# Merge stage of a hybrid decoder step: gates and projections as seven quarter products instead of eight

## The chip, the cores and the metric

The kernel runs on one core of a Trainium2 chip. The metric is the device time of one execution in microseconds. Everything is float32.

## The reference, cut to what matters

The program is one step of a decoder trunk with two branches, RWKV-7 time mixing and sparse attention, over 1024 prompt tokens and 8 sample tokens. The change concerns how the two branches are merged:

```
zs, zg_r, q, ..., zg_n, mg = split_in(rmsnorm(h, norm_g) @ w_in)      # mg: 2 x 1024 columns
g_r, g_n = split(sigmoid(mg), 2)
m = g_r * ((o_r * silu(zg_r)) @ proj_r) + g_n * ((o_n * silu(zg_n)) @ proj_n)   # proj_*: 512 x 1024
h = h + m @ w_out                                                     # w_out: 1024 x 1024
e = rmsnorm(p @ w_pe, pe_norm_g)
h = h + sigmoid(h @ w_pg) * e
```

## The kernel before, in words

Stages follow each other in one program, each with a queue of instructions written out by hand for each engine (SyncE issues the loads); semaphores order them, and a stage begins when all engines have ended the one before.

Activations lie transposed in on-chip memory, features on the 128 partitions and the 1032 tokens (TT, 1024 prompt and 8 sample) along the row: `xnT` (8 blocks of 128 features, the normalized input), `zgr` and `zgn` (4 blocks each, parts of `zT`, the gated outputs of the two branches), `mT` (8 blocks, the merged result). When the merge stage begins, `mT` holds the first gate g_r, which earlier stages computed between their own matmuls. Such a stage, `attend_sample`, also issues the first two loads of merge weights.

`merge_branches` goes over 8 blocks f of 128 output features and, in each, over three thirds of 344 tokens (CG): 24 units u. A unit has 16 matmuls on TensorE: 8 for the second gate (line 2666, weights `wm` from w_in, moving operand `xnT`), 4 for each projection (line 2670, weights `wp`). ScalarE takes the sigmoid of the gate (L2680), VectorE multiplies each projection with its gate from PSUM (L2690), GpSimd adds the two into `mT` (L2707). Two sets of PSUM banks alternate. SyncE loads the weights of block f + 2 (one load of 512 KB, one of 256, two of 128) when block f is summed, and behind the first of these the 4 MB of `w_out`. After units 15, 17 and 19 VectorE makes sums of w_out's quarters (`w_sums`, L2694 to L2700).

`finish_tokens`, the last stage, computes m @ w_out and h @ w_pg for pairs of token tiles, already each as seven products of quarters (P1 to P7, in the order P1, P5, P6, P2, P7, P3, P4) for eight. A product is 4 float32 matmuls of 512 columns (L2823). The operand sums of the tokens (`sums`, in `ring_k`) and of the weights are VectorE's work. The stage opens with `sample_out` (L2907), 64 narrow records of the 8 sample tokens; behind it come the seven products of pair 0. The residual additions (L3131) read a product from PSUM, and P6, P7 and P4 wait for the additions before them, since they add into the same bank.

Of the kernel before, what the change touches and what calls it, by code (L numbers as in the profile page):

```python
# [14 lines left out]
ALU = mybir.AluOpType  # L15
# [2185 lines left out]
def load_merge_weights(sp, k, x, f):  # L2201

    s, cols = f % 2, slice(f * P, (f + 1) * P)
    w_rows = x.w_in[0].rearrange("(c p) n -> p c n", p=P)
    r_rows = x.proj_r[0].rearrange("(c p) n -> p c n", p=P)
    n_rows = x.proj_n[0].rearrange("(g j d) n -> g d j n", g=2, d=HD)
    sp.dma_start(k.wm[:, s], w_rows[:, :, OFF_MGN + f * P:OFF_MGN + (f + 1) * P]).then_inc(k.in_merge_w[s], 16)
    sp.dma_start(k.wp[:, s, 0], r_rows[:, :, cols]).then_inc(k.in_merge_w[s], 16)
    for g in range(2):
        sp.dma_start(k.wp[g * HD:(g + 1) * HD, s, 1], n_rows[g, :, :, cols]).then_inc(k.in_merge_w[s], 16)  # L2210


def attend_sample(nc, k, x):
# [5 lines left out]
    with Stage(nc) as ctx:  # L2219
# [57 lines left out]
        def _(sp):  # L2277
# [16 lines left out]
            for f in range(2):  # L2294
                load_merge_weights(sp, k, x, f)
# [335 lines left out]
def merge_branches(nc, k, x):  # L2631

    ring = 2
    with Stage(nc) as ctx:
        wm, wp, in_w = k.wm, k.wp, k.in_merge_w
        free = k.zT[:, 8:10, :].rearrange("p a t -> p (a t)")
        sg = free[:, 0:2 * CG].rearrange("p (s t) -> p s t", s=2)
        tt = free[:, 2 * CG:6 * CG].rearrange("p (s n t) -> p s n t", s=2, n=2)  # L2640
        in_wo = ctx.sem("in_w_out")
        summed, sigd, termed, added, made = (ctx.sem(n) for n in ("m_summed", "m_sig", "m_terms", "m_added", "w_out_sums"))
        block = ctx.enter_context(nc.Block())
        lo, hi, left, right = slice(0, 4), slice(4, 8), slice(0, 512), slice(512, D)

        @block.sync
        def _(sp):
            for f in range(ring, KC):
                sp.wait_ge(summed, 3 * (f - ring + 1))
                load_merge_weights(sp, k, x, f)  # L2650
                if f == ring:
                    sp.dma_start(k.w_out[:], x.w_out[0].rearrange("(c p) n -> p c n", p=P)).then_inc(in_wo, 16)
            sp.wait_ge(in_wo, 16)

        @block.tensor
        def _(pe):
            for f in range(KC):
                s = f % ring
                pe.wait_ge(in_w[s], 64 * (f // ring + 1))
                for g in range(3):  # L2660
                    u, cs = 3 * f + g, slice(g * CG, (g + 1) * CG)
                    b = 4 * (u % 2)
                    if u >= 2:
                        pe.wait_ge(termed, 2 * (u - 1))
                    for c in range(KC):
                        nc.tensor.matmul(k.ps[:, b + 1, 0:CG], wm[:, s, c, :], k.xnT[:, c, cs],  # L2666
                                         start=(c == 0), stop=(c == KC - 1))
                    for n, src in enumerate((k.zgr, k.zgn)):
                        for c in range(NPAIR):
                            last = nc.tensor.matmul(k.ps[:, b + 2 + n, 0:CG], wp[:, s, n, c, :], src[:, c, cs],  # L2670
                                                    start=(c == 0), stop=(c == NPAIR - 1))
                    last.then_inc(summed, 1)

        @block.scalar
        def _(act):
            for u in range(3 * KC):
                act.wait_ge(summed, u + 1)
                if u >= 2:
                    act.wait_ge(termed, 2 * (u - 1))
                nc.scalar.activation(sg[:, u % 2], k.ps[:, 4 * (u % 2) + 1, 0:CG], ACT.Sigmoid).then_inc(sigd, 1)  # L2680

        @block.vector
        def _(dve):
            for u in range(3 * KC):
                dve.wait_ge(sigd, u + 1)
                if u >= 2:
                    dve.wait_ge(added, u - 1)
                gates = (k.mT[:, u // 3, u % 3 * CG:(u % 3 + 1) * CG], sg[:, u % 2, :])
                for n in range(2):
                    nc.vector.tensor_tensor(tt[:, u % 2, n, :], k.ps[:, 4 * (u % 2) + 2 + n, 0:CG], gates[n],  # L2690
                                            ALU.mult).then_inc(termed, 1)
                if u == 15:
                    dve.wait_ge(in_wo, 16)
                    nc.vector.tensor_tensor(k.wt[:, 0], k.w_out[:, lo, right], k.w_out[:, lo, left], ALU.subtract).then_inc(made, 1)  # L2694
                if u == 17:
                    dve.wait_ge(made, 1)
                    nc.vector.tensor_tensor(k.wt[:, 1], k.w_out[:, hi, right], k.wt[:, 0], ALU.subtract).then_inc(made, 1)
                if u == 19:
                    dve.wait_ge(made, 2)
                    nc.vector.tensor_tensor(k.wt[:, 2], k.w_out[:, hi, left], k.wt[:, 1], ALU.subtract).then_inc(made, 1)  # L2700

        @block.gpsimd
        def _(pool):
            for u in range(3 * KC):
                f, g = u // 3, u % 3
                pool.wait_ge(termed, 2 * (u + 1))
                nc.gpsimd.tensor_tensor(k.mT[:, f, g * CG:(g + 1) * CG], tt[:, u % 2, 0, :], tt[:, u % 2, 1, :],  # L2707
                                        ALU.add).then_inc(added, 1)


PRODUCTS = ("P1", "P5", "P6", "P2", "P7", "P3", "P4")


def finish_tokens(nc, k, x, o):
# [8 lines left out]
    with Stage(nc) as ctx:  # L2723
# [3 lines left out]
        wo, wot, wg, we = k.w_out, k.wt, sb("w_pg", [P, KC, D]), sb("w_pe", [P, 2, D])  # L2727
# [20 lines left out]
        s_made, t3_made, tg_made = ctx.sem("operand_sums"), ctx.sem("w_out_t3"), ctx.sem("w_pg_sums")  # L2748
# [70 lines left out]
        def _(pe):  # L2819
# [7 lines left out]
            def out_product(name, p):  # L2827
                if name == "P1" and p >= 2:
                    pe.wait_ge(h_out, 7 * (p - 1))
                elif name == "P5":  # L2830
                    pe.wait_ge(s_made, 4 * p + 1)
                    if p:
                        pe.wait_ge(h_out, 7 * p - 1)
                elif name == "P6":
                    pe.wait_ge(s_made, 4 * p + 2)
                    pe.wait_ge(h_out, 7 * p + 1)
                elif name == "P7":
                    pe.wait_ge(s_made, 4 * p + 3)
                    pe.wait_ge(h_out, 7 * p + 3)
                    pe.wait_ge(t3_made, 1)  # L2840
                elif name == "P3":
                    pe.wait_ge(s_made, 4 * p + 4)
                elif name == "P4":
                    pe.wait_ge(h_out, 7 * p + 5)
                product(name, p).then_inc(h_ps, 1)
# [261 lines left out]
        def _(dve):  # L3107
# [57 lines left out]
            def sums_of_gate_weights(n):  # L3165
                if n == 0:
                    nc.vector.tensor_tensor(wot[:, 0], wg[:, 0:4, cols(1)], wg[:, 0:4, cols(0)], ALU.subtract).then_inc(tg_made, 1)
                elif n == 1:
                    dve.wait_ge(tg_made, 1)
                    nc.vector.tensor_tensor(wot[:, 1], wg[:, 4:8, cols(1)], wot[:, 0], ALU.subtract).then_inc(tg_made, 1)  # L3170
                elif n == 2:
                    dve.wait_ge(tg_made, 2)
# [218 lines left out]
```

## Time and profile before

| | us |
|---|---|
| runs of the kernel before | 1857.47, 1858.22, 1869.94 |
| median | 1858.22 |
| profiled execution, its time | 1855.13 |
| its span, first to last instruction | 1853.0 |
| mean granted TensorE clock, share of full | 0.974 |
| merge stage, TensorE's first to last record | 1370.04 to 1594.05 |

Times in the trace are microseconds from the start of the span. PE is TensorE's matmuls, PEld its weight loads (they overlap PE), DVE VectorE, ACT ScalarE, POOL GpSimd, SP SyncE; PEq and SPq are sequencers. A float32 matmul stands as two records. L2666 is line 2666 of the kernel.

### The profile page before, as it was taken

Reading aid. Unit: us, or ns where it says so; the run is one execution under the profiler, and the core shown is the slowest. Engines: PE = TensorE matmul, PEld = TensorE weight load, DVE = VectorE, ACT = ScalarE, POOL = GpSimd, SP = SyncE. Lnnn points to the kernel's source line nnn. Section 1 sums busy time; section 2 is a strip of 40 time slices with the busy share of each in tenths; the row PEclk is TensorE's granted clock in tenths of the full one; section 3 lists DMA queues with packets and bytes.
Section 4 is the critical chain, followed back from the end, with each engine's and each line's share of the span. In section 5 each row is a group of like instructions: output and inputs, shape, how many; then the busy total and the mean of one; then the engine's idle time right before and its main releaser. Section 6 shows DMA issues by size and latency. Waiting matters only on the chain. (4 is left out here: it accounts for less than half of the span.)

```text
span 1853.0 us, 40230 instructions
## 1 busy us (share of the span) xinstructions
PE 1729.4 (93%) x17720; PEld 1141.5 (62%) x17720; DVE 750.0 (40%) x1520; ACT 545.7 (29%) x1145; POOL 385.6 (21%) x438
## 2 busy tenths in 40 slices
PE   7999899999999899799888599899999999999997
PEld 5666566666666555666666489776656666545443
DVE  3101255555554262366666566172111111323444
ACT  4111344344432101465666021222310000011344
POOL 0111232222221000154444321112200011000112
PEclk9999899999999999799999799999999999999999
DMA  4111000000001161460000597538624010410001
GB/s 153 46 35 51 2 14 15 14 17 23 14 14 26 51 119 23 115 171 1 2 2 1 224 288 264 181 99 198 151 46 136 23 46 23 179 72 1 23 23 45
DMA packets 115026, 135.82 MB, mean 73 GB/s; under 512 B 48204, under 2 KB 97045, under 8 KB 110286
## 3 DMA queue, kind: packets, MB, share of 16 engines
q1 hardware_dynamic: 105536, 83.95, 16.3%
q0 software_dynamic: 9216, 49.29, 8.6%
q8 instruction: 140, 2.29, 0.5%
q14 instruction: 32, 0.26, 0.0%
q10 hardware_dynamic: 102, 0.03, 0.0%
HBM read 120.64 MB, written 16.62 MB: 74 GB/s over the span
## 5 line engine op out<-in xcount | busy, mean ns | idle before, releaser
L725 PE MATMUL ps<-xnT,rw_side_w 128*128 128x344 f32 x576 | 204.5, 479 | 0.0
L443 PE MATMUL ps<-xnT,w_z 128*128 128x344 f32 x624 | 184.2, 457 | 2.3 <-DVE xnT L537 1.3
L443 PEld LDWEIGHTS ps<-xnT,w_z 128*128 128x128 f32 x624 | 119.3, 192 | 63.9 <-issue 3.3
L1928 POOL TENSOR_SCALAR probs<-probs,row_sums,gates 128x63 f32<-128x63 f32 (+6 forms) x148 | 95.0, 657 | 260.7 <-DVE row_sums L1888 260.7
L725 PEld LDWEIGHTS ps<-xnT,rw_side_w 128*128 128x128 f32 x576 | 99.5, 191 | 40.4 <-issue 3.6
L2180 PE MATMUL ps<-xnT,zT 128*128 128x344 f32 x384 | 121.4, 465 | 0.0
L2666 PE MATMUL ps<-xnT,ring_k 128*128 128x344 f32 x384 | 116.7, 458 | 2.2 <-PEq L81 2.2
L2670 PE MATMUL ps<-zT,ring_k 128*128 128x344 f32 x384 | 115.0, 452 | 0.0
L2666 PEld LDWEIGHTS ps<-xnT,ring_k 128*128 128x128 f32 x384 | 73.8, 192 | 41.2 <-issue 4.0
L2670 PEld LDWEIGHTS ps<-zT,ring_k 128*128 128x128 f32 x384 | 73.0, 190 | 38.0
L2180 PEld LDWEIGHTS ps<-xnT,zT 128*128 128x128 f32 x384 | 72.1, 195 | 36.2 <-issue 6.0
L256 PE MATMUL ps<-w_kv,xnT 128*128 128x396 f32 x256 | 89.0, 510 | 4.6 <-DMA w_kv<-in_w_in_dram 4.6
L2690 DVE TENSOR_TENSOR zT<-ps,mT 128x344 f32<-128x344 f32 x24 | 12.4, 516 | 197.7 <-ACT zT L2680 197.7
L1797 PE MATMUL ps<-ident,probs 128*128 128x128 f32 (+1 forms) x460 | 70.4, 283 | 20.1 <-ACT probsT L1853 11.1
L1837 ACT ACTIVATE probs<-probs,neg_max 128x63 f32<-128x63 f32 (+6 forms) x148 | 87.5, 595 | 3.3 <-DVE neg_max L1878 3.3
L2707 POOL TENSOR_TENSOR mT<-zT 128x344 f32<-128x344 f32 x24 | 27.9, 1161 | 244.1 <-DVE zT L2690 244.1
L256 PEld LDWEIGHTS ps<-w_kv,xnT 128*128 128x128 f32 x256 | 49.4, 194 | 43.9 <-DMA w_kv<-in_w_in_dram 8.9
L1784 PE MATMUL ps<-kT,zT 64*128 64x512 f32 (+3 forms) x384 | 73.8, 497 | 2.4 <-PEq L81 1.1
L1853 ACT ACTIVATE probsT<-ps 128x512 f32<-128x512 f32 (+1 forms) x80 | 45.9, 574 | 100.7 <-PE ps L1797 100.2
L2680 ACT ACTIVATE zT<-ps 128x344 f32<-128x344 f32 x24 | 11.0, 457 | 215.3 <-PE ps L2670 215.3
L1797 PEld LDWEIGHTS ps<-ident,probs 128*128 128x128 f32 (+1 forms) x460 | 50.7, 142 | 35.3 <-issue 17.4
L1811 PE MATMUL ps<-probsT,kvtok 128*64 128x128 f32 x1056 | 71.8, 281 | 0.5 <-ACT probsT L1853 0.5
(531 smaller groups left out, 3000.0 us busy)
## 6 DMA issues: line engine op xcount, KB each, us to landing
w_z<-in_w_in_dram SPq DMA_DIRECT2D x13, 512.0 KB, 3.7
xnT_kept<-xnT SPq DMA_DIRECT2D x1, 4128.0 KB
xnT<-xnT_kept SPq DMA_DIRECT2D x1, 4128.0 KB, 13.6
x_tok<-in_x_prompt_dram SPq DMA_DIRECT2D x8, 512.0 KB, 5.7
rw_side_w<-in_w_in_dram SPq DMA_DIRECT2D x16, 256.0 KB, 3.3
zT<-in_w_in_dram SPq DMA_DIRECT2D x8, 512.0 KB, 5.9
ring_k<-in_w_in_dram SPq DMA_DIRECT2D x8, 512.0 KB, 3.9
w_out<-in_w_out_dram SPq DMA_DIRECT2D x1, 4096.0 KB
```

The source lines that it names most:

```text
L256: last = nc.tensor.matmul(k.ps[:, u % 4, 0:half], k.xnT[:, c, i * P:(i + 1) * P], w[:, c, h * half:(h + 1) * half], start=(c == 0), stop=( ...
L443: last = nc.tensor.matmul(k.ps[:, u % 6, 0:CG], w[:, n % w_ring, c, :], k.xnT[:, c, g * CG:(g + 1) * CG], start=(c == 0), stop=(c == KC - 1))
L725: ins = nc.tensor.matmul(k.ps[:, SIDE_BANKS[g % 2], 0:CG], w.side[:, t % 2, c, :], k.xnT[:, c, g % 3 * CG:(g % 3 + 1) * CG], start=(c == 0 ...
L1784: last = nc.tensor.matmul(k.ps[:, 2 * (s % 2) + g, at:at + w], k.qT[half(g), j, i * P:(i + 1) * P], keys[half(g), t0:t0 + w], start=True, ...
L1797: last = nc.tensor.transpose(k.ps[0:m, 4 + pc % 2, (2 * b + g) * P:(2 * b + g + 1) * P], region(n, br, g, t * P, m), k.ident[:])
L1811: last = nc.tensor.matmul(k.ps[half(g), 6 + n % 2, 0:P], vals, pt[0:m, pc % NPT, (2 * b + g) * P:(2 * b + g + 1) * P], start=(br == 1 and ...
L1837: nc.scalar.activation(every, every, ACT.Exp, scale=-1.0, bias=neg_m[:, at:at + 1], accum_out=ls[:, at:at + 1]).then_inc(expd, 1)
L1853: nc.scalar.activation(to, src, ACT.Copy).then_inc(pt_a, 1)
L1928: nc.gpsimd.tensor_scalar(every, every, ls[:, at:at + 1], k.gates[:, i, gate:gate + 1], ALU.mult, ALU.mult).then_inc(scaled, 1)
L2180: ins = self.nc.tensor.matmul(self.k.ps[:, self.banks[n % nb], 0:CG], self.w[:, t % 2, c, :], self.k.xnT[:, c, g * CG:(g + 1) * CG], start ...
L2666: nc.tensor.matmul(k.ps[:, b + 1, 0:CG], wm[:, s, c, :], k.xnT[:, c, cs], start=(c == 0), stop=(c == KC - 1))
L2670: last = nc.tensor.matmul(k.ps[:, b + 2 + n, 0:CG], wp[:, s, n, c, :], src[:, c, cs], start=(c == 0), stop=(c == NPAIR - 1))
```

## The change

The merge stage is split in two by time, and both parts use quarters.

- Gates first, for all features: four units, one for each pair of feature blocks (p, p + 4). Input features, output features and tokens are each cut in two: of the inputs 4 blocks and 4 blocks, of the outputs block p and block p + 4, and of the tokens each half of 516 into two quarters of CQ = 258. Seven products of quarters stand for eight; each is 4 matmuls of 258 columns, and is made for both token halves i. This is one round r of 14 product groups.
- Then both projections: four units of two rounds (n = 0: proj_r, n = 1: proj_n), each again 7 products for both halves, but with 2 matmuls in each, since a projection has 4 input blocks.
- The second gates are kept, in a new buffer `gate_n` of 7 blocks and a free place in `zT`; a projection's results are multiplied in place with `mT` (n = 0) or `gate_n` (n = 1), and GpSimd adds the two in the rounds n = 1.
- ScalarE copies three intermediate sums of each round from PSUM (`held`), VectorE adds them to the later products; ScalarE takes the sigmoids in the gate rounds.
- VectorE makes the sums of weights (`operand_sum`, 4 of 512 columns a unit), of inputs (`input_sum`, 4 of 2064 columns, before the first round) and of the branches (`branch_sums`, 8 of 1032 columns in the fourth round).
- Weights load in pairs of blocks, 1 MB a unit. `w_out`, whose memory holds the input sums, is loaded only after the gate rounds.
- The three sums of w_out move from the merge stage to the last stage, where the buffer `w_sums` now lives; with the fourth, which was there already, they are made in order: two before sample_out is awaited, one behind it, one after P6's residual of pair 0.

```
+CQ = TT // 4
+MERGE_UNITS, GATE_UNITS = 8, 4
+MERGE_ROUNDS = GATE_UNITS + 2 * (MERGE_UNITS - GATE_UNITS)
...
+            for u in range(2, MERGE_UNITS):
+                sp.wait_ge(summed, 14 * (last_round(u - 2) + 1))
+                load_merge_pair(sp, k, x, u)
+                if u == GATE_UNITS + 1:
+                    sp.wait_ge(summed, 14 * GATE_UNITS)
                     sp.dma_start(k.w_out[:], x.w_out[0].rearrange("(c p) n -> p c n", p=P)).then_inc(in_wo, 16)
...
         @block.tensor
+            for r in range(MERGE_ROUNDS):
+                u, n = unit_of(r)
+                if n == 0:
+                    pe.wait_ge(in_w[u % 2], merge_landed(u))
+                for name in PRODUCTS:
+                    for i in range(2):
+                        bank = {"P2": 4 + i, "P5": 6 + i, "P3": 6 + i}.get(name, bank_a(r, i))
+                        if name == "P1":
+                            if 2 <= r < GATE_UNITS + 2:
+                                pe.wait_ge(sigd, 8 * (r - 2) + 7 + i)
+                            elif r >= GATE_UNITS + 2:
+                                pe.wait_ge(gated, 8 * (r - 2 - GATE_UNITS) + 7 + i)
+                        elif name == "P5":
+                            pe.wait_ge(s_made, 4 * u + 1)
+                            pe.wait_ge(tx_made if r < GATE_UNITS else tz_made, 1 if r < GATE_UNITS else 2)
+                            if r:
+                                pe.wait_ge(added, 6 * (r - 1) + 5 + i)
...
+                        else:
+                            pe.wait_ge(tx_made if r < GATE_UNITS else tz_made, 4 if r < GATE_UNITS else 8)
+                            pe.wait_ge(added, 6 * r + 3 + i)
+                        tiles = 4 if u < GATE_UNITS else 2
+                        for c in range(tiles):
+                            last = nc.tensor.matmul(k.ps[:, bank, 0:CQ], stationary(u, n, name, c), moving(u, n, name, c, i),
+                                                    start=(c == 0 and name in ("P1", "P5", "P2")), stop=(c == tiles - 1),
+                                                    skip_group_check=True)
+                        last.then_inc(summed, 1)
...
         @block.scalar
+                for b, bank in enumerate((bank_a(r, 0), 6, bank_a(r, 0))):
+                    for i in range(2):
+                        act.wait_ge(summed, 14 * r + 2 * b + i + 1)
...
+                        nc.scalar.activation(held[:, b, i, :], k.ps[:, bank + i, 0:CQ], ACT.Copy).then_inc(copied, 1)
...
         @block.vector
+            def finished(r, b):
+                u, n = unit_of(r)
+                j, h = ((0, 0), (1, 1), (0, 1), (1, 0))[b]
+                for i in range(2):
+                    dve.wait_ge(summed, 14 * r + (7, 9, 11, 13)[b] + i)
+                    f, q = u % 4 + 4 * j, held[:, min(b, 2), i, :]
+                    part = k.ps[:, (4 + i, bank_a(r, i), 6 + i, bank_a(r, i))[b], 0:CQ]
+                    gate = k.mT[:, f, columns(i, h)] if n == 0 else gate_block(f, i, h)
+                    if b < 3:
+                        dve.wait_ge(copied, 6 * r + (1, 3, 5)[b] + i)
+                        to = q if r >= GATE_UNITS else gate_block(f, i, h)
+                        nc.vector.tensor_tensor(to, part, q, ALU.add).then_inc(added, 1)
+                        part = q
+                        if r >= GATE_UNITS:
+                            dve.wait_ge(added, 6 * r + 2 * b + i + 1)
+                    if r >= GATE_UNITS:
...
+                        nc.vector.tensor_tensor(gate, part, gate, ALU.mult).then_inc(gated, 1)
...
+            for r in range(MERGE_ROUNDS):
+                u, n = unit_of(r)
+                more = r == last_round(u) and u + 1 < MERGE_UNITS
+                if r == GATE_UNITS - 1:
+                    branch_sums(0, 2, 0)
+                    branch_sums(2, 2, 2)
+                finished(r, 0)
+                if r == GATE_UNITS - 1:
+                    branch_sums(1, 8, 2)
+                if more:
+                    operand_sum(u + 1, 0)
+                    operand_sum(u + 1, 1)
+                finished(r, 1)
...
         @block.gpsimd
+            for r in range(GATE_UNITS + 1, MERGE_ROUNDS, 2):
+                u, n = unit_of(r)
+                for b, (j, h) in enumerate(((0, 0), (1, 1), (0, 1), (1, 0))):
+                    for i in range(2):
+                        f = u % 4 + 4 * j
+                        pool.wait_ge(gated, 8 * (r - GATE_UNITS) + 2 * b + i + 1)
+                        to = k.mT[:, f, columns(i, h)]
+                        nc.gpsimd.tensor_tensor(to, to, gate_block(f, i, h), ALU.add).then_inc(joined, 1)
...
 def finish_tokens(nc, k, x, o):
             operand_sums(0)
+            weight_sums(wo, 0, to_made)
+            weight_sums(wo, 1, to_made)
             dve.wait_ge(sh_ps, 1)
-            nc.vector.tensor_tensor(wo[:, 0:4, cols(1)], wo[:, 4:8, cols(1)], wo[:, 0:4, cols(1)], ALU.subtract).then_inc(t3_made, 1)
+            weight_sums(wo, 2, to_made)
...
                 residual(p, 3, 0, 1, a, True)
+                if p == 0:
+                    weight_sums(wo, 3, to_made)
```

## Rows read from the trace of the kernel before

**Rows 1.** The page's summary: busy us, share of the span and instructions by engine.
```profile
PE 1729.4 (93%) x17720; PEld 1141.5 (62%) x17720; DVE 750.0 (40%) x1520; ACT 545.7 (29%) x1145; POOL 385.6 (21%) x438
```

**Rows 2.** TensorE in time, merge stage: start, length, records, idle before.
```profile
1370.04 6.56 PE L2666 MATMUL ps<-xnT,ring_k 128*128 128x344 f32 x16 [2.18 <-PEq L81]
...
1381.06 4.79 PE L2666 MATMUL ps<-xnT,ring_k 128*128 128x344 f32 x16
...
1589.26 4.79 PE L2670 MATMUL ps<-zT,ring_k 128*128 128x344 f32 x16
```

**Rows 3.** Stretches: engines' busy time, then granted clock, DMA share, GB/s.
```profile
1370.00:1594.00 224.00, 223.97 (x768) 146.86 (x768) 28.17 (x49) 10.51 (x23) 26.95 (x23) 0.99 0.17 47
...
1370.00:1376.00 6.00, 5.96 (x15) 3.76 (x16) 0.00 (x0) 0.00 (x0) 0.00 (x0) 0.72 0.01 4
...
1594.00:1600.00 6.00, 2.76 (x29) 1.53 (x32) 3.01 (x8) 0.46 (x1) 1.44 (x5) 0.72 0.03 10
```

**Rows 4.** TensorE in time, last stage.
```profile
1597.28 5.02 PE L2907 MATMUL ps<-w_out,mT 128*32 128x256 f32 x64 [3.24 <-PEq L81]
...
1605.77 7.03 PE L2823 MATMUL ps<-w_sums,ring_k 128*128 128x512 f32 x16
...
1625.27 3.60 PE L2823 MATMUL ps<-w_sums,mT 128*128 128x512 f32 x8
...
1723.53 3.60 PE L2823 MATMUL ps<-w_pg,mT 128*128 128x512 f32 x8
...
1747.57 3.60 PE L2823 MATMUL ps<-w_sums,ring_k 128*128 128x512 f32 x8
1752.17 3.67 PE L2823 MATMUL ps<-w_sums,ring_k 128*128 128x512 f32 x8 [1.01 <-ACT w_out L3003]
```

**Rows 5.** TensorE in time, small matmuls with full weights.
```profile
1252.97 1.00 PE L2395 MATMUL ps<-s_win,ones 128*128 128x64 f32 x8
```

**Rows 6.** All engines in time, merge stage.
```profile
1521.40 2.28 DVE L2694 TENSOR_TENSOR w_sums<-w_out 128x2048 f32<-128x2048 f32 x1
1521.56 2.89 POOL L2707 TENSOR_TENSOR mT<-zT 128x344 f32<-128x344 f32 x1 [8.34 <-DVE zT L2690]
...
1594.57 0.52 DVE L2690 TENSOR_TENSOR zT<-ps,mT 128x344 f32<-128x344 f32 x1 [8.32 <-ACT zT L2680]
...
1595.59 0.91 POOL L2707 TENSOR_TENSOR mT<-zT 128x344 f32<-128x344 f32 x1 [8.34 <-DVE zT L2690]
```

**Rows 7.** VectorE in time, start of the last stage.
```profile
1599.41 0.68 DVE L3118 TENSOR_TENSOR ring_k<-mT 128x512 f32<-128x512 f32 x1
1600.02 0.68 DVE L3120 TENSOR_TENSOR ring_k<-ring_k,mT 128x512 f32<-128x512 f32 x1
1600.73 0.69 DVE L3122 TENSOR_TENSOR ring_k<-mT,ring_k 128x512 f32<-128x512 f32 x1
1602.36 2.29 DVE L3184 TENSOR_TENSOR w_out<-w_out 128x2048 f32<-128x2048 f32 x1 [0.94 <-PE ps L2907]
...
1605.97 0.69 DVE L3131 TENSOR_TENSOR h_tok<-ps,h_tok 128x512 f32<-128x512 f32 x1 [0.98 <-PE ps L2823]
...
1616.27 0.69 DVE L3131 TENSOR_TENSOR h_tok<-ps,h_tok 128x512 f32<-128x512 f32 x1 [2.74 <-PE ps L2823]
```

**Rows 8.** ScalarE and GpSimd in time, 256 columns, last stage.
```profile
1629.93 0.38 ACT L3055 ACTIVATE squares_s<-ps 128x256 f32<-128x256 f32 x1 [10.09 <-PE ps L2934]
...
1659.12 0.73 POOL L3094 TENSOR_TENSOR y_sample<-y_sample,g_pe_s 128x256 f32<-128x256 f32 x1 [61.35 <-DVE y_sample L3216]
```

**Rows 9.** DMA in 1390 to 1430: GB/s in 40 slices, issues and landing.
```profile
GB/s 0 0 0 0 0 0 0 0 0 0 18 263 331 294 235 342 414 401 401 426 410 418 377 414 410 90 16 0 0 0 0 0 0 0 0 0 0 0 49 287
...
ring_k<-in_w_in_dram SPq DMA_DIRECT2D x2, 512.0 KB, 3.9
```

**Rows 10.** VectorE in time, 512 columns beside additions of GpSimd.
```profile
1742.85 1.64 DVE L3154 TENSOR_TENSOR h_tok<-w_out,h_tok 128x512 f32<-128x512 f32 x1
1744.96 1.21 DVE L3152 TENSOR_TENSOR w_out<-w_out 128x512 f32<-128x512 f32 x1 [0.47 <-ACT w_out L3022]
```

More of the change, by code:

```diff
@@ new lines, in gate_block, with weights, sums_of @@
+        def gate_block(f, i, h):
+            tile = gate_n[:, f, :] if f < KC - 1 else place[:, 0:TT]
+            return tile[:, columns(i, h)]
+        def weights(u, j, half):
+            if u < GATE_UNITS:
+                return wq[:, u % 2, j, 4 * half:4 * half + 4, :]
+            return wq[:, u % 2, j].rearrange("p (n c) m -> p n c m", n=2)[:, :, 2 * half:2 * half + 2, :]
+        def sums_of(u, q):
+            if u < GATE_UNITS:
+                return sums[:, q, :].rearrange("p (c m) -> p c m", m=P)
+            return sums[:, q, :].rearrange("p (n c m) -> p n c m", n=2, m=P)
@@ new lines, in branch_sum, with branch, stationary @@
+        def branch_sum(q, n):
+            rows = slice(2 * n, 2 * n + 2)
+            return (xv[:, rows, :, 0, :], xv[:, 4 + 2 * n:6 + 2 * n, :, 0, :], zv[:, 4 * n:4 * n + 2, :, 1, :],
+                    xv[:, rows, :, 1, :])[q]
+        def branch(n, half, h):
+            return zv[:, 4 * n + 2 * half:4 * n + 2 * half + 2, :, h, :]
+        def stationary(u, n, name, c):
+            j, half = {"P1": (0, 0), "P2": (0, 1), "P4": (1, 1)}.get(name, (None, None))
+            if j is None:
+                q = {"P5": 0, "P6": 1, "P7": 2, "P3": 3}[name]
+                at = (c if u < GATE_UNITS else 2 * n + c) * P
+                return sums[:, q, at:at + P]
+            return wq[:, u % 2, j, 4 * half + c if u < GATE_UNITS else 4 * n + 2 * half + c, :]
@@ L2682, in _, with operand_sum @@
         @block.vector
         def _(dve):
[L2684 to L2688, printed above, removed]
-                for n in range(2):
[L2690 to L2700, printed above, removed]
+            def operand_sum(u, q):
+                if q == 0:
+                    dve.wait_ge(in_w[u % 2], merge_landed(u))
+                if u:
+                    dve.wait_ge(summed, 14 * last_round(u - 1) + (4, 6, 10, 12)[q])
+                if q == 1 or q == 3:
+                    dve.wait_ge(s_made, 4 * u + q - (q == 3))
+                one, other, op = ((weights(u, 1, 0), weights(u, 1, 1), ALU.add), (sums_of(u, 0), weights(u, 0, 0), ALU.subtract),
+                                  (weights(u, 0, 0), weights(u, 1, 0), ALU.subtract),
+                                  (weights(u, 0, 1), sums_of(u, 1), ALU.subtract))[q]
+                nc.vector.tensor_tensor(sums_of(u, q), one, other, op).then_inc(s_made, 1)
@@ new lines, in _ @@
+            for q in range(4):
+                operand_sum(0, q)
+                input_sum(q)
+            for r in range(MERGE_ROUNDS):
+                u, n = unit_of(r)
[10 more added lines that the diff above has]
+                finished(r, 1)
+                if r == GATE_UNITS - 1:
+                    branch_sums(3, 10, 6)
+                if more:
+                    operand_sum(u + 1, 2)
+                finished(r, 2)
+                if more:
+                    operand_sum(u + 1, 3)
+                if r >= GATE_UNITS:
+                    finished(r, 3)
```

176 lines of the change are left out of this document (105 added, 71 removed).

## The prediction, made before the changed kernel ran

> **What bounds the kernel now.** I read the summary first: TensorE has work for 93% of the span, no other engine for more than 40% [rows 1]. Then the matmul timeline of the merge stage [rows 2]: after a slow start the blocks of 16 records follow each other every 4.63 us, with no idle note, until the last block ends at 1589.26 + 4.79 = 1594.05. The table by stretches says the same, 223.97 us busy in 224.00, while VectorE works 28.2 us, ScalarE 10.5 and GpSimd 27.0 [rows 3]. So the stage is as long as its matmul stream, and helpers matter only where TensorE has to wait for them. A float32 matmul leaves two records. From 1381.06 to 1589.26 lie 45 blocks of 16, 208.20 us / 720 = 289.2 ns per record of 344 columns.
>
> **What a record of 258 columns takes.** The trace has none. Records of 512 columns stand 429.3 ns apart (1723.53 to 1747.57, 56 records) [rows 4]. Between 344 and 512 that is 140.1 / 168 = 0.834 ns per column, two passes at the 2.4 GHz level, with 2.5 ns left over. 258 columns: 289.2 - 86 x 0.834 = 217.5 ns. This holds only if the weight load still hides. A load shows as 190 ns, of full weights, but 8 records of 64 columns with fresh 128x128 weights fit in 1.00 us, 125 ns each at most [rows 5]. That is the nearest row to a floor, and it is well below 217.5. I take 217.5; ends 216 and 222.
>
> **The matmul sum.** Before: 24 units (8 feature blocks, 3 token thirds) of 16 matmuls, 768 records, 222.1 us. After: four gate rounds of 7 products x 2 halves x 4 tiles are 224 matmuls, eight projection rounds of 7 x 2 x 2 are 224 more; 896 records x 217.5 = 194.9 us. **Term 1: -27.2 us.** (12.5% fewer columns; the fixed 2.5 ns per record is paid 128 times more often, 0.3 us.)
>
> **The start of the stage.** The first 16 records took 6.56 us, later ones 4.79 [rows 2], at a granted clock of 0.72 [rows 3]; the idle before them was 2.18 us. This 1.8 us stays. New in front of it are VectorE's sums: four of 512 columns and four of 2064, in turn. By rows of 0.69 us (0.61 start to start when nothing is waited for, 0.71 when the one before is) and 2.28 for 2048 [rows 6, 7], P5's operands are there at 0.7 + 2.3 = 3.0, P6's at 6.1, P7's at 9.0 and P4's at 12.1. TensorE asks for them at 3.5 to 5.3, 8.8, 15.7 and 22.7 (each product 16 x 217.5 = 3.48, plus the slow start). Nothing is paid; cover 0.5 us at worst.
>
> **Gate rounds (24.4 us each).** VectorE has 6 additions from PSUM. A 344-column one is 0.516, a 512-column one 0.69 [rows 6, 7], so 258 columns are about 0.43; with four weight sums, 5.3 us a round. P7's half is ready at 15.7, P4 of that half wants its bank back at 20.9. ScalarE's six copies (0.38 each by a 256-column row [rows 8]) and eight sigmoids of that size make 5.3 us of 24.4, and the sigmoids are wanted only two rounds later. In the fourth round come eight branch sums of 1032 columns, 1.23 each: four between 3.5 and 8.4, two from 13.9, with two weight sums and P7's addition after them at 18.4 against 20.9 needed; then two more and the rest until 23.5, before P5 of the next round wants anything at 26.1. Nothing is paid. DMA: as before 1 MB per pair of blocks, asked for a whole unit (24.4 us) ahead, where a landing takes 3.9 us; w_out (4 MB) moves from the first third to the middle, about 97 us before it is needed, and took some 15 us (slices 11 to 25, of 1 us) [rows 9]. What is queued behind the later wait on SyncE is only the next pair, not due before another 24 us. Nothing.
>
> **Projection rounds (56 records, 12.2 us each).** Here product and half are two matmuls, 0.87 us, and the margins shrink. Counted from the round's start, P2 halves end at 6.1 and 7.0, P7 at 7.8 and 8.7; P4 wants its banks at 10.4 and 11.3, which needs the additions of P7. VectorE from 7.0 on: add 0.43, multiply 0.41, in the second round of a unit two sums of the next weights (1.3), then P7's first add, done near 9.6. Margin 0.8 us. P5 of the next round (13.9, 14.8) needs P3's additions, done near 12 and 13. Without further trouble nothing is paid.
>
> The further trouble is GpSimd. In the second round of each unit it adds eight pairs of 258 columns, both in SBUF, just while VectorE multiplies and sums SBUF by SBUF. The trace shows that these hold each other up: a GpSimd addition of 344 columns is 0.91 alone but 2.89 when it is issued 0.16 us into VectorE's 2048-column sum, and it ends 0.77 after that sum [rows 6]. It works the other way too: VectorE's 512-column additions take 1.21 to 1.64 instead of 0.69 beside GpSimd [rows 10]. A GpSimd addition of 258 columns is about 0.73 [rows 8]. One of them falling between 7.0 and 10.4 uses the margin, two overrun it by 0.7. Three rounds (the second ones of the first three units) have both kinds of work, so between 0 and, with the same again at P5, 3 x 1.4 = 4.2 us. Most orders of arrival give one such wait before P7's addition. **Term 2: +1.0 us (0 to 4.2).**
>
> The Trainium skill has this as a rule ("SBUF — State Buffer", the section on the two separate sides): the port pair of VectorE and GpSimd is an exclusive lock for a whole instruction, also taken by a VectorE operation with two SBUF inputs. By that rule, the trace agrees in both directions; it turns the margin of a mean into one of an order, and it is what rival B prices from the rows.
>
> **The end of the stage.** Before: sigmoid, two products, GpSimd's sum of 0.91; from the last matmul's end (1594.05) to the next stage's first (1597.28) 3.24 us, of which 0.78 after GpSimd [rows 4, 6]. After: one multiply from PSUM (0.47 with its wait) and the sum (0.08 + 0.73), so 1.3 + 0.8 = 2.1 at the least. GpSimd comes with a backlog: eight sums become due between 7.0 and 12.7, and each can be held 0.41 by a multiply; at 1.14 each until VectorE falls silent it is done about 2.5 after the last matmul, 3.3 in all. I take 2.8. **Term 3: -0.4 us (-1.1 to +0.5).**
>
> **The last stage.** It inherits four sums of 2048 columns; one (L3184) was there already. VectorE now does the two first ones after its operand sums (1601.3 on): 1603.6 and 1605.9; the third, which must wait for sample_out's end at 1602.3, ends at 1608.2 instead of 1604.65; behind it stand the h_sample addition (256 columns, about 0.4) and the first residual, which ends at 1609.2 instead of 1606.66 [rows 7]. P5 (1605.77) has what it needs since 1603.6. P6 would start at 1609.2 (1605.77 + 8 x 0.429) [rows 4] and waits for that residual: 0 to 0.2 us. The fourth sum falls into the idle 2.7 us ahead of 1616.27 and is not wanted before P4, at 1625 [rows 4, 7]. Removed from the merge stage, the three sums save nothing, since they stood beside matmuls. **Term 4: +0.1 us (0 to 1).**
>
> **Sum.** -27.2 + 1.0 - 0.4 + 0.1 = -26.5. The profiled execution took 1855.13 (span 1853.00 and 2.1 around it), so 1828.6 for a profiled one. The median of the three runs is 1858.22, 3.1 above; the forecast is 1858.22 - 26.5, about 1831.7. About 1% (18.6 us) is what a measurement here can tell from no change; faster by more ends at 1839.6.
>
> **Rivals.**
> A, my forecast: dense stream, terms as above. Terms 2 to 4 at their good ends give -28.3 (1829.9), record ends of 216 ns another 1.3; all bad ends -21.5. Chance 0.68, own range 1827 to 1835.
>
> B: the hold-ups between VectorE and GpSimd decide the projection rounds. If every sum of GpSimd costs VectorE its full 0.73, a second round holds 8 x 0.43 + 6 x 0.41 + 4 x 0.65 + 8 x 0.73 = 14.3 us for VectorE, against 12.2 of matmuls: +2.1 in four rounds, 8.4, with the end at +0.5 and the last stage at +0.5. -27.2 + 9.4 = -17.8, 1840.4. For it: the held operations of [rows 6, 10]. Against: half of VectorE's operations read PSUM and were not held in any row here, and the first rounds, with 5.9 us of VectorE work, take up arrears. Chance 0.17, 1835 to 1843.
>
> C, slower: TensorE's clock. After an idle of 2.18 us the next 6 us ran at 0.72, and 0.72 again after 3.24 [rows 2, 3]; after 1.01 us in the last stage eight records took 3.67 against 3.60 [rows 4]. Should P4 in each of twelve rounds wait over 2 us for VectorE's additions, each time costs 2.2 of waiting and 1.8 of slow records, 48 us: -27 + 48 = +21, 1879. It decides from waits of about 2 us on, in more than half of the rounds; at my margins (0.8) waits of 0.7 are in sight, not 2. Chance 0.05.
>
> D: many short groups cost TensorE something. There are 112 groups of four records with up to three waits each. In the last stage groups of eight with up to three waits run at the plain 429 ns [rows 4], no row has groups of four. 0.05 us each would give +5.6, 1837; 0.25 each would eat the gain, 1859. Chance 0.07, 1837 to 1859.
>
> E: it does not do what it says, because something else was the limit of the stage, a load for example. The stream without idle [rows 2] speaks against it; 0.03, about 1855.
>
> Range for 8 in 10: A and most of B, 1827 to 1841. Faster by over 1%: A, three quarters of B, under half of D, 0.68 + 0.13 + 0.03 = 0.84. Within 1%: the rest of B, half of D, and E, 0.11. Slower: C, 0.05.
>
> **What the new profile would show.** Record spacing in the stage of 217.5 ns, blocks of eight records 1.74 us apart (217 right; 250 or more: the load does not hide, and term 1 is wrong). The first P5 without an idle note. In projection rounds, idle of TensorE put down to VectorE ahead of P4 or P5, in rounds 5, 7 and 9 only (term 2), under 1 us each; in all rounds, B or C. VectorE multiplies and GpSimd sums above 0.41 and 0.73 where they overlap. The gap from the last merge matmul to sample_out between 2.1 and 3.3. P6 of the first output pair at most 0.2 late, P4 on time. A granted clock below 0.95 anywhere inside the stage but at its start would make the prediction wrong, and so would a first P1 held by its loads.

## The result, and the profile after

The changed kernel took 1828.26 us, the median of 4 runs (1827.45 to 1845.88), against 1861.76 of 4 runs of the kernel before (1857.47 to 1869.94). The ratio is 0.9852, with a 95% interval from 0.9811 to 0.9892: faster by 1.5%. Timed again on another occasion (last experiment), 1836.05 of 6 runs stand against 1857.12 of 11, ratio 0.9894, from 0.9861 to 0.9927. The two intervals overlap, and neither holds 1. The forecast started from 1858.22, the median of three of the four runs of the kernel before. The profiled execution took 1828.42 us, its span is 1826.6.

First the summary and the slices of the changed kernel's page; the slices show where in the span an engine is busy, in tenths.

```profile
PE 1701.3 (93%) x17848; PEld 1164.6 (64%) x17848; DVE 825.5 (45%) x1652; ACT 575.4 (32%) x1225; POOL 384.3 (21%) x446
...
PEld 5666566666666645566666388876668888545443
```

Beside [rows 1], matmuls are busy 28.1 us less in spite of 128 more instructions, weight loads 23 us more, VectorE 75.5 more, ScalarE 29.7 more. In the slices of the merge stage weight loads stand at 8 tenths (before at 6). The helpers' work cost nothing where they had time.

TensorE in time, from the merge stage's start into the last stage; it answers to [rows 2, 4]. What stands in brackets is called the idle note: how long the engine sat idle before these records, and what ended it.

```profile
1370.08 5.41 PE L2766 MATMUL ps<-xnT,ring_k 128*128 128x258 f32 x16 [2.18 <-PEq L81]
1375.32 7.12 PE L2766 MATMUL ps<-w_out,zT 128*128 128x258 f32 x32
...
1469.28 1.90 PE L2766 MATMUL ps<-zT,ring_k 128*128 128x258 f32 x8
1471.02 3.64 PE L2766 MATMUL ps<-xnT,zT 128*128 128x258 f32 x16
...
1488.42 3.64 PE L2766 MATMUL ps<-zT 128*128 128x258 f32 x16
1491.97 1.98 PE L2766 MATMUL ps<-xnT,ring_k 128*128 128x258 f32 x8
1493.78 1.90 PE L2766 MATMUL ps<-zT,ring_k 128*128 128x258 f32 x8
...
1565.39 1.90 PE L2766 MATMUL ps<-xnT,ring_k 128*128 128x258 f32 x8
1570.59 3.66 PE L3082 MATMUL ps<-w_out,mT 128*32 128x256 f32 x64 [3.29 <-PEq L81]
...
1577.72 3.60 PE L2995 MATMUL ps<-w_sums,ring_k 128*128 128x512 f32 x8
1582.73 3.67 PE L2995 MATMUL ps<-w_sums,ring_k 128*128 128x512 f32 x8 [1.42 <-DVE h_tok L3306]
```

Four things are to be seen. From 1375.32 to 1469.28 lie 27 blocks of 16 with no idle note: 3.48 us each, 217.5 ns per record. The first block, 5.41 for 3.64, shows the slow start, 1.8 us as before. P4 of round 5 starts at 1491.97, 0.07 after it would follow (1488.42 + 3.48), and its block takes 1.81 us instead of 1.74. And idle notes stand only ahead of the last stage (3.29) and, new, at P6 of pair 0, released by VectorE's L3306; it is 1.58 us late (1577.72 + 3.43 = 1581.15). An idle note counts from the modelled end of the record before and so shows 1.42. The stage's stretch and the last stage's first 3.59 us, by busy time and granted clock, answer to [rows 3]:

```profile
1370.08:1567.29 197.21, 197.21 (x896) 170.88 (x896) 97.03 (x178) 40.64 (x104) 24.36 (x29) 0.99 0.18 54
```

```profile
1570.59:1574.18 3.59, 3.59 (x64) 2.36 (x65) 2.91 (x8) 0.00 (x0) 0.49 (x4) 1.00 0.26 46
```

The way to compare the two profiles is by stage, since executions differ before the change begins: TensorE's first merge record stands at 1370.04 before and 1370.08 here, but between 1373.5 and 1381.9 in the eight other profiles of the changed kernel or a variant of it, whose code up to there is the same. So the whole time carries up to 12 us that arise before the stage; from the merge stage's start to the end the changed kernel's two profiles agree to 0.1 us (456.52, and 456.59 in the last experiment). Of the kernel before there is one profile, so whether it reaches the stage at another time on average is not shown.

| us | before | after | difference |
|---|---|---|---|
| merge stage, first to last record | 224.01 | 197.21 | -26.80 |
| from there to sample_out | 3.23 | 3.30 | +0.07 |
| last stage to the end | 255.72 | 256.01 | +0.29 |
| sum | 482.96 | 456.52 | -26.44 |

One difference in it is not the change's for certain: `sample_out`, with which the last stage opens, took 4.95 us before (1597.28 [rows 4] to 1602.23) at a granted clock of 0.72, and 3.59 after at 1.00. At the full clock the profile of the kernel before would be up to 1.36 us shorter, and the sum could shrink to -25.1 from -26.4 (an estimate from these two durations).

### The profile page after: what moved, and what is told of

It reads as the page before. It is cut to its first block and busy times, and to the rows that moved or that the text cites. A ratio compares the mean times of both kernels' runs of the same rounds, so it can differ in the third digit from the quotient of the medians.

```text
span 1826.6 us, 40926 instructions
## 1 busy us (share of the span) xinstructions
PE 1701.3 (93%) x17848; PEld 1164.6 (64%) x17848; DVE 825.5 (45%) x1652; ACT 575.4 (32%) x1225; POOL 384.3 (21%) x446
## 5 line engine op out<-in xcount | busy, mean ns | idle before, releaser
L562 DVE SCALAR_TENSOR_TENSOR zT<-z_diff,vec,zT 128x1032 f32<-128x1032 f32 x13 | 16.8, 1293 | 126.2 <-POOL z_diff L417 113.5
L1811 PEld LDWEIGHTS ps<-probsT,kvtok 128*64 128x64 f32 x1056 | 57.1, 138 | 21.5 <-issue 19.6
L1909 DVE COPY probsT<-ps 128x512 f32<-128x512 f32 (+1 forms) x80 | 50.7, 634 | 44.4 <-PE ps L1797 44.4
L2883 POOL TENSOR_TENSOR mT<-mT,gate_n 128x258 f32<-128x258 f32 x28 | 23.7, 852 | 218.0 <-DVE gate_n L2846 218.0
L1224 POOL TENSOR_TENSOR rw_Lb<-rw_Lm,level_mask 128x512 f32<-128x512 f32 x40 | 53.9, 1357 | 62.4 <-DVE rw_Lm L1393 38.8
L2782 ACT ACTIVATE zT<-ps 128x258 f32<-128x258 f32 x72 | 27.8, 386 | 109.0 <-PE ps L2766 86.3
L2995 PE MATMUL ps<-w_sums,ring_k 128*128 128x512 f32 x128 | 57.3, 595 | 4.5 <-ACT w_out L3178 3.0
```

The lines of the kernel that those rows point to most:

```text
L1224: nc.gpsimd.tensor_tensor(w.Lb[:, n % 2], w.Lm[:].rearrange("p q c n -> p (q c) n"), bc(k.tab["level_mask"][:, n + 1, :], 1, 8), ALU.mult) ...
L1811: last = nc.tensor.matmul(k.ps[half(g), 6 + n % 2, 0:P], vals, pt[0:m, pc % NPT, (2 * b + g) * P:(2 * b + g + 1) * P], start=(br == 1 and ...
L1909: nc.vector.tensor_copy(to, src).then_inc(pt_v, 1)
L2995: last = nc.tensor.matmul(k.ps[:, bank, :], left[:, c, :], right[:, c, :], start=(first and c == 0), stop=(c == 3), skip_group_check=True)
```

## The experiments

### The missing eighth put back

```
-                        for c in range(tiles):
+                        for c in [c for _ in range(2 if name == "P2" else 1) for c in range(tiles)]:
```

> The changed kernel with the product P2 issued twice in every round, the second time over the first, so that every round has eight products; all helper work, the order of gates and projections and the loads are those of the changed kernel. Theory (the gain is the missing eighth of the matmul stream): 64 matmuls and so 128 records more, 128 x 217.5 ns = 27.8 us; the profiled time goes from 1828.4 to about 1856.2, within 1 us of the kernel before (1855.1), and the merge stage from 197.2 to 225.0 us. Rival (a part of the gain comes from gates before projections, smaller tiles or the moved sums): the time ends more than 3 us below that of the kernel before. Rival 2 (helpers bind in the projection rounds): the longer rounds hide something, and less than 25 us is added.

Measured: 1859.52 (10 runs) against 1859.69 (13 runs) of the kernel before, ratio 0.999, from 0.997 to 1.0011. The profiled execution took 1861.32 and not the expected 1856.2; it reached the stage 5.7 us later than the changed kernel's, so the stage decides. TensorE in time, its start and the start of the next:

```profile
1375.79 5.41 PE L2766 MATMUL ps<-xnT,ring_k 128*128 128x258 f32 x16 [2.18 <-PEq L81]
...
1603.52 3.66 PE L3082 MATMUL ps<-w_out,mT 128*32 128x256 f32 x64 [3.08 <-PEq L81]
```

The stage took 224.64 us (1375.79 to 1603.52 less the gap of 3.08), 27.43 more than without the eighth product; from its start to the end 483.71, against 482.96 before. The 128 records more would be 27.84 us at 217.5 ns; 0.41 is missing because P4 does not wait in this run (term 2 below). With eight products the whole change is worth +0.75 us: that is the price of its helpers, shorter matmuls, moved sums. Of it 0.63 lies in the stage, where 1024 records of 217.5 ns for 768 of 289.2 make 0.6; against a profile of the kernel before at the full clock in sample_out the price would be up to 2.1 (the same estimate). Both rivals fall. This is the cleanest evidence of where the gain comes from: not from gates before projections, nor from smaller tiles, but from an eighth of the stream.

### The third sum of w_out later

```
-            dve.wait_ge(sh_ps, 1)
-            weight_sums(wo, 2, to_made)
             for p in range(NPR):
                 residual(p, 1, 0, 0, a, True)
+                if p == 0:
+                    dve.wait_ge(sh_ps, 1)
+                    weight_sums(wo, 2, to_made)
```

(and the h_sample addition with it)

> The changed kernel, but VectorE makes the third sum of w_out (and the h_sample addition) after the first residual of pair 0 instead of before it. Theory (in the last stage P6 waits 1.42 us for that residual, which stands behind three sums of 2048 columns): the wait at P6 goes, P6 starts at P5's start + 3.43, and everything behind it comes 1.4 us earlier, unless the clock is down at the stage's start, when there was no such wait to begin with and the gain is 0.2. Rival (the next in line is as late: the load of p for the small transposes, or P7, whose operand is this third sum): the wait only moves to the transposes after P2 or to P7, and nothing is gained.

VectorE in time, in the changed kernel and then in this one:

```profile
1574.65 2.28 DVE L3347 TENSOR_TENSOR w_sums<-w_out 128x2048 f32<-128x2048 f32 x1
1576.96 2.29 DVE L3347 TENSOR_TENSOR w_sums<-w_out,w_sums 128x2048 f32<-128x2048 f32 x1
1579.36 2.29 DVE L3347 TENSOR_TENSOR w_out<-w_out 128x2048 f32<-128x2048 f32 x1
...
1581.91 0.68 DVE L3306 TENSOR_TENSOR h_tok<-ps,h_tok 128x512 f32<-128x512 f32 x1
```

```profile
1590.99 0.68 DVE L3306 TENSOR_TENSOR h_tok<-ps,h_tok 128x512 f32<-128x512 f32 x1
1591.59 2.28 DVE L3347 TENSOR_TENSOR w_out<-w_out 128x2048 f32<-128x2048 f32 x1
```

TensorE in this one, whose P5 and P6 are one block again:

```profile
1582.40 3.66 PE L3082 MATMUL ps<-w_out,mT 128*32 128x256 f32 x64 [3.29 <-PEq L81]
...
1589.53 7.03 PE L2995 MATMUL ps<-w_sums,ring_k 128*128 128x512 f32 x16
1596.39 3.60 PE L2995 MATMUL ps<-w_out,mT 128*128 128x512 f32 x8
```

The residual that P6 waits for ends 9.27 us after the stage's start instead of 12.00, the wait at P6 is gone, and nothing takes its place: transposes and P7 follow without an idle note. The last stage takes 254.40 instead of 256.01. The theory holds, the rival doesn't. The median of this kernel, 1837.61 against 1859.69 (ratio 0.9883, from 0.9858 to 0.9909), shows nothing of this, because this execution reached the merge stage 11.8 us later than the changed kernel's: an effect of 1.6 us is to be read from the stage.

### GpSimd's additions left out, and made twice

Out in rounds 5, 7 and 9:

```
-            for r in range(GATE_UNITS + 1, MERGE_ROUNDS, 2):
+            for r in range(MERGE_ROUNDS - 1, MERGE_ROUNDS, 2):
```

> The changed kernel without GpSimd's additions in rounds 5, 7 and 9 (three quarters of the merged result lack the second branch); only the last unit is added. Theory (a GpSimd addition and a VectorE operation with two on-chip-memory inputs hold each other): in rounds 5, 7 and 9 the second weight sum falls from 1.03 to 0.69 us, multiplies from 0.66-0.73 to 0.43, and the idle of 0.07 us ahead of P4 goes; the merge stage is 0.2 us shorter. Rival (the durations are of dependence on the operation before, or of PSUM access): they stay as they are.

Twice (with a semaphore between the two):

```
+                        nc.gpsimd.tensor_tensor(place[:, TT + 6 * CQ:TT + 7 * CQ], to, gate_block(f, i, h), ALU.add).then_inc(twice, 1)
                         nc.gpsimd.tensor_tensor(to, to, gate_block(f, i, h), ALU.add).then_inc(joined, 1)
```

> The changed kernel with each of GpSimd's additions made twice, the first into a scratch place. Theory (hold-ups by GpSimd are what eats VectorE's margin ahead of P4): twice as many operations of 0.73 us between 7.0 and 10.4 us of the odd projection rounds hold VectorE longer, and P4 waits 0.3 to 1.5 us in rounds 5, 7 and 9 instead of 0.07; the end of the stage comes some 3 to 6 us later, since GpSimd's sixteen additions of the last round take at least 11.7 us from about 7 us on. Rival (each VectorE operation is held at most once, by the one GpSimd operation in progress, and GpSimd was already busy there): the wait ahead of P4 stays under 0.3 us and only the end of the stage moves.

Each of the two ran once; they are read from the stage and from durations, not from their whole times (1838.07 and 1840.17).

All engines in time, the changed kernel, round 5 around P4:

```profile
1489.67 0.68 DVE L2807 TENSOR_TENSOR zT<-ring_k 128x512 f32<-128x512 f32 x1
1489.82 1.11 POOL L2883 TENSOR_TENSOR mT<-mT,gate_n 128x258 f32<-128x258 f32 x1 [0.36 <-DVE gate_n L2846]
1490.45 1.03 DVE L2807 TENSOR_TENSOR zT<-zT,ring_k 128x512 f32<-128x512 f32 x1
1491.41 0.41 DVE L2839 TENSOR_TENSOR zT<-ps,zT 128x258 f32<-128x258 f32 x1
...
1491.97 1.98 PE L2766 MATMUL ps<-xnT,ring_k 128*128 128x258 f32 x8
```

The same place on VectorE without GpSimd:

```profile
1498.38 0.68 DVE L2807 TENSOR_TENSOR zT<-ring_k 128x512 f32<-128x512 f32 x1
1499.17 0.69 DVE L2807 TENSOR_TENSOR zT<-zT,ring_k 128x512 f32<-128x512 f32 x1
1499.78 0.42 DVE L2839 TENSOR_TENSOR zT<-ps,zT 128x258 f32<-128x258 f32 x1
```

And with the additions made twice, VectorE and then TensorE:

```profile
1493.75 1.21 DVE L2808 TENSOR_TENSOR zT<-ring_k 128x512 f32<-128x512 f32 x1
1495.07 1.03 DVE L2808 TENSOR_TENSOR zT<-zT,ring_k 128x512 f32<-128x512 f32 x1
1496.03 0.41 DVE L2840 TENSOR_TENSOR zT<-ps,zT 128x258 f32<-128x258 f32 x1
```

```profile
1496.59 1.98 PE L2767 MATMUL ps<-xnT,ring_k 128*128 128x258 f32 x8 [0.43 <-DVE zT L2840]
...
1521.62 1.98 PE L2767 MATMUL ps<-xnT,ring_k 128*128 128x258 f32 x8 [0.43 <-DVE zT L2840]
...
1546.65 1.98 PE L2767 MATMUL ps<-xnT,ring_k 128*128 128x258 f32 x8 [0.43 <-DVE zT L2840]
...
1581.29 6.37 PE L3085 MATMUL ps<-w_out,mT 128*32 128x256 f32 x64 [8.30 <-PEq L81]
```

Read the durations: the second weight sum takes 1.03, 0.69, 1.03 us, the first one 0.68, 0.68, 1.21, while additions from PSUM stay at 0.41 to 0.43 in all three. P7's first addition ends at 1491.82 in the changed kernel, P4 would be due at 1491.90 and starts at 1491.97, 0.15 after that addition's end (in the run with the additions made twice it is 0.15 too, 1496.44 to 1496.59). With the longer block behind it that is 0.13 to 0.14 us in each of three rounds, 0.41. Without GpSimd in these rounds the stage takes 196.80 us, 0.41 less than 197.21: the whole of it, and twice the 0.2 that was expected. With twice its work P4 is 0.60 late each time (idle notes of 0.43) and the stage takes 198.82, and GpSimd's sixteen additions of the last round hold the next stage back to 8.30 us after the last matmul. The mechanism is shown from both sides; its size is small, since two additions of GpSimd held a multiply by 0.23 (0.66 us for 0.43) and a weight sum by 0.34, while VectorE without them was done 0.65 ahead of P4 (1500.20 against 1500.85).

### Fewer columns

```
+                            w = CQ if c == 0 and name in ("P1", "P5", "P2") else 129
-                            last = nc.tensor.matmul(k.ps[:, bank, 0:CQ], stationary(...), moving(...),
+                            last = nc.tensor.matmul(k.ps[:, bank, 0:w], stationary(...), moving(...)[:, 0:w],
```

> The changed kernel, in which every merge matmul but the first of P1, P5 and P2 of each half has 129 columns instead of 258 (half of each quarter of tokens gets only a part of its sum). One size is changed, to ask what holds a record when the columns no longer do. Theory (the two passes over the columns set the spacing, the weight load hides): 129 x 0.834 + 2.5 = 110 ns between narrow records; a gate round falls from 24.4 to 12 x 217.5 + 100 x 110 ns = 13.6 us. Rival (the weight load of 190 ns becomes the limit): 190 ns or more, a gate round of 21.6 us. In the projection rounds the matmuls fall to 7.5 us, while VectorE's work there was 6.5 us in a first round and 9.5 in a second one: there the stage becomes VectorE's, P4 waits in every second round, and the pair of rounds takes 16 to 18 us instead of 24.4.

The other with 64 in the place of 129:

> As the run with 129 columns, with 64. Theory (columns alone): 64 x 0.834 + 2.5 = 56 ns between narrow records. Rival (a floor of the weight load, of the rows with 64 columns of the kernel before at most 125 ns): 100 to 125 ns, the same in a gate round as with 129 columns.

Both leave out a part of the sums, and each ran once. TensorE in time with 129 columns, a gate round, then projection rounds:

```profile
1393.34 2.37 PE L2767 MATMUL ps<-xnT,ring_k 128*128 128x258 f32 x16
...
1401.76 3.74 PE L2767 MATMUL ps<-xnT,zT 128*128 128x129 f32 x32
1405.33 1.95 PE L2767 MATMUL ps<-w_out,ring_k 128*128 128x129 f32 x16
1407.12 2.37 PE L2767 MATMUL ps<-xnT,ring_k 128*128 128x258 f32 x16
...
1449.43 1.95 PE L2767 MATMUL ps<-zT 128*128 128x129 f32 x16
1453.19 1.48 PE L2767 MATMUL ps<-xnT,ring_k 128*128 128x129 f32 x8 [1.81 <-DVE zT L2840]
...
1471.23 1.48 PE L2767 MATMUL ps<-xnT,ring_k 128*128 128x129 f32 x8 [1.80 <-DVE zT L2840]
```

With 64 columns:

```profile
1388.79 7.03 PE L2767 MATMUL ps<-xnT,zT 128*128 128x64 f32 x32
...
1414.43 2.37 PE L2767 MATMUL ps<-xnT,ring_k 128*128 128x258 f32 x16
...
1422.85 3.74 PE L2767 MATMUL ps<-xnT,zT 128*128 128x64 f32 x32
1426.42 1.95 PE L2767 MATMUL ps<-w_out,ring_k 128*128 128x64 f32 x16
1428.21 2.37 PE L2767 MATMUL ps<-xnT,ring_k 128*128 128x258 f32 x16
```

Narrow records stand (1405.33 - 1401.76) / 32 = 111.6 ns apart with 129 columns, and (1426.42 - 1422.85) / 32 = 111.6 with 64; gate rounds last 13.78 us in both. So 64 columns gain nothing over 129, as the rival for 64 said: that is the floor with fresh full weights, 111.6 ns, although a load shows as 190. At 129 columns theory (110) and floor meet; 258 are far above it. In the projection rounds P4 waits 1.8 us in every second round and a pair takes 18.04 us (1453.19 to 1471.23), just above the expected 16 to 18: there the stage is VectorE's. In the run with 64 columns the blocks from 1376.80 to 1402.86 ran at a granted clock of 0.50 to 0.52, the lower of the two levels (7.03 us for 32 records against 3.74), with no idle note among them, and three places in the projection rounds at 0.59 to 0.67. Its stage took 145.52 us against 129.89 with 129 columns, where the clock was 0.99 from 1380.93 to 1430, and its whole time, 1782.47, is above 1771.48. The spacing of 111.6 ns is read where the clock was 1.00; why it stayed low is open.

### Three edits of order together, beside the changed kernel again

The third sum late, as above; and

```
                 if more:
                     operand_sum(u + 1, 0)
-                    operand_sum(u + 1, 1)
+                    if r < GATE_UNITS:
+                        operand_sum(u + 1, 1)
                 finished(r, 1)
+                if more and r >= GATE_UNITS:
+                    operand_sum(u + 1, 1)
```

and the last round's two additions of P4's results on VectorE instead of GpSimd.

> The changed kernel with three edits of order: the third sum of w_out after the first residual (as in the run with the late third sum, 1.6 us less from the last stage's start to the end), the second weight sum of a unit after P7's additions instead of before them in the projection rounds (takes away the 0.07 us ahead of P4 in three rounds, 0.2 us), and in the last round the additions of P4's halves on VectorE instead of GpSimd (GpSimd ended 2.5 us after the last matmul, VectorE 1.0; by the durations 1.9 for both, 0.5 us less). Theory: 2.3 us less than the changed kernel from the merge stage's start to the end, 456.5 to 454.2. Rival (the end of the stage is bound by VectorE and GpSimd holding each other, so that moving two additions gains nothing): 454.7 to 455. The whole time differs by several us between executions before the merge stage begins, so that the interval of the median may not show it.

> The changed kernel once more, on the same chip as the run with the three edits of order, for the comparison. Theory: from the merge stage's start to the end 456.5 us as before or, where the first matmuls of the last stage run at the lower clock (sample_out over 5 us instead of 3.66), 457.5 to 458; between its median and that of the kernel before 26 to 28 us. Rival (part of the first measured difference of 33 us between the medians is the change's): 30 us or more.

TensorE in time, first the three edits, then the changed kernel:

```profile
1380.61 5.41 PE L2766 MATMUL ps<-xnT,ring_k 128*128 128x258 f32 x16 [2.18 <-PEq L81]
...
1579.94 5.22 PE L3091 MATMUL ps<-w_out,mT 128*32 128x256 f32 x64 [2.53 <-PEq L81]
1585.09 3.70 PE L3004 MATMUL ps<-w_out,mT 128*128 128x512 f32 x8
1588.63 7.03 PE L3004 MATMUL ps<-w_sums,ring_k 128*128 128x512 f32 x16
```

```profile
1373.51 5.41 PE L2766 MATMUL ps<-xnT,ring_k 128*128 128x258 f32 x16 [2.18 <-PEq L81]
...
1574.03 3.66 PE L3082 MATMUL ps<-w_out,mT 128*32 128x256 f32 x64 [3.30 <-PEq L81]
...
1586.19 3.67 PE L2995 MATMUL ps<-w_sums,ring_k 128*128 128x512 f32 x8 [1.44 <-DVE h_tok L3306]
```

Each edit shows at its own place: the stage takes 196.80 instead of 197.22 us, the gap after it 2.53 instead of 3.30, and P6 doesn't wait. From the merge stage's start to the end it is 455.69 against 456.59, 0.9 less and not 2.3 (454.2 was expected, 454.7 to 455 by the rival, and neither came), mainly because here sample_out ran at a granted clock of 0.69 and took 5.15 us instead of 3.59. Medians: 1836.65 (ratio 0.9877, from 0.9847 to 0.9908) and 1836.05 (0.9894, from 0.9861 to 0.9927), not to be told apart. Shown is a version faster by parts of the trace, not one that is faster by the clock on the wall. As to the first difference between medians, 33.5 us, this time it is 21.1: neither 26 to 28 nor 30 and more. The stage difference, 26.4, lies between them, and the changed kernel's profile repeats it (456.59, 456.52).

## Why the prediction was right

It forecast 1831.7, in a range from 1827 to 1841; both medians, 1828.26 and 1836.05, lie in it. The working was for a profiled execution, 1828.6, and the profiled one took 1828.42; the sum was -26.5 and the stages give -26.44. That close an agreement is partly luck. Small terms were off both ways; the two profiled executions happened to reach the merge stage within 0.04 us of each other, where others of the same code came up to 12 us later; and the two medians lie 3.4 below and 4.4 above the forecast. What the traces bear out is the mechanism and the size of the stage's change.

- **Term 1, -27.2.** Records of 258 columns: 217.5 ns forecast from the rows of 344 and 512 columns, 217.5 measured. The weight load hides, with 106 ns to spare against the floor that the two runs with fewer columns found. The run with eight products gave 27.4 us for the missing eighth. (The 2.5 ns left over in the working is 2.3 by its own 0.834; the 217.5 does not hang on it.)
- **Term 2, +1.0.** Measured 0.41: 0.13 to 0.14 in rounds 5, 7 and 9, at the place and in the rounds named. The mechanism was right and the term sized too large. P7's first addition, forecast at 9.6 us with a margin of 0.8, ended at 10.36 (1491.82, the round starting at 1481.46): the hold-ups used up the margin and little more. Two additions of GpSimd fall into the stretch, as feared, but an operation of VectorE waits only for what is left of one in progress, 0.23 and 0.34, not 0.73. At P5 nothing was lost. With -27.2 this gives the stage's -26.8.
- **Start of the stage.** Nothing paid, as said. P5's operands were there 2.9 us in (forecast 3.0), and it began 5.2 in.
- **Gate rounds, loads.** No idle of TensorE in them; w_out's later load was in time.
- **Term 3, -0.4.** Measured +0.07. The least (2.1) would have needed helpers without backlog; VectorE ended its last multiply 0.98 us after the last matmul, GpSimd its last two additions 2.48 after (the estimate was 2.5), and with 0.82 behind it the gap is 3.30. The 2.8 of the prediction, between the two, had no row for it; the working's own 3.3 was the answer.
- **Term 4, +0.1.** Measured +0.29, and for another reason than forecast. P6's time after the stage's start was forecast as bound by VectorE's three sums: 11.9 to 12.1 us, measured 12.14, before 11.92. But the forecast had P6 at most 0.2 late, and it is 1.58 late behind P5. The working had not seen that sample_out could be 1.36 us shorter (3.59 for 4.95), and that P6, bound by VectorE, would give it all back; the moved sums cost more than the +0.29 shows. The experiment with the late third sum shows that VectorE was the bound there, since it gained 1.61 without anything else in its way.
- **Rivals.** B's mechanism is in the trace, its price isn't: multiplies of 0.51 to 0.73 and sums of 1.03 where GpSimd is at work, but operations that read PSUM are not held (0.41 to 0.43), and first rounds are not touched (multiplies 0.43). C didn't come (granted clock 1.00 from 1376 to the end of the stage). D didn't: groups of four records with three waits ran at 217.5 ns too. E fell with the run of eight products.

## What to carry to other kernels

Where one engine streams without a gap and a trace has its instruction at two sizes, the price of a third size can be read to the nanosecond, as long as it stays above the floor; what is uncertain is the half microsecond in which a helper hands back a bank, and that is decided by the order of a few instructions, not by the helpers' busy share. Replace the products of such a stream by seven for eight as long as a record stays clear of the floor (here 111.6 ns, about 129 columns) and a round stays longer than VectorE's work in it. And compare by stage: a change of 1.4% was plain from the stage's start to the end, to a few tenths once sample_out's clock (1.4 us) is told apart, while two pairs of medians gave 33.5 and 21.1 us.

## What was not expected of the hardware

- The clock after the gap ahead of the last stage is not settled by the gap. After 3.29 us (changed kernel), 3.08, 3.29 and 3.30 (eight products, late third sum, changed kernel again) sample_out took 3.59 us; after 3.24 (before), 3.31 (GpSimd's last unit only) and a shorter one of 2.53 (three edits) it took 4.95, 6.36 and 5.15, at granted clocks of 0.72, 0.55 and 0.69: means of two levels, 0.5 and 1.0 (1.2 and 2.4 GHz). After the longer gaps of 4.82, 5.11 and 8.30 (64 columns, 129 columns, GpSimd twice) it took 5.83, 6.50 and 6.30. What decides between them after gaps of 3.1 to 3.3 stays open; it is worth up to 2.8 us there, and more than the edits that were tried.
- A float32 record with fresh full weights has a floor of 111.6 ns with 64 as with 129 columns, though each weight load shows as 190 ns.
- A VectorE operation with both inputs in on-chip memory and an addition of GpSimd hold each other. The Trainium skill says so of the shared port pair ("SBUF — State Buffer", the section on the two separate sides: it names VectorE operations with two SBUF inputs); the trace agrees, with 0.69 against 1.03 us for a sum of 512 columns. An operation with one input from PSUM is not held: 0.41 to 0.43 throughout for the additions from PSUM, with GpSimd's work, without it and with twice as much.
- The time until the merge stage starts varied from 1370.0 to 1381.9 us between profiles with the same code up to there. It arises at more than one place: at the matmul of L201 the profiles stand at 740.4 to 748.9 us, and the run with the late third sum, 11.8 us late at the stage, was at 741.1 there. The cause was not pursued.
